# Feed-forward borders rearranged, and the up stage's weight sums made by VectorE

## The chip, the cores and the metric

The kernel runs on one core of a Trainium2 chip. The metric is the device time of one execution in microseconds (us): 1914.89, the median of 3 runs (1914.2 to 1916.0). The core has TensorE (PE), VectorE (DVE), ScalarE (ACT), GpSimd (POOL) and SyncE (SP); here SP issues nearly all transfers.

## The reference

One transformer block over x (2048 x 1024, float32): a mixer (windowed attention with sinks beside a gated spatial unit) and a SwiGLU feed-forward, each between two RMS norms. The change touches the border between the two and the feed-forward (D_FF is 2816):

```python
        mix = jnp.concatenate([rms_norm(a_out, norm_out_attn[l]),
                               rms_norm(s_out, norm_out_sgu[l])], axis=-1) @ w_out[l]
        x = x + rms_norm(mix, norm_mix_post[l])
        f = swiglu(rms_norm(x, norm_ffn_pre[l]), w_gate[l], w_up[l], w_down[l])
        x = x + rms_norm(f, norm_ffn_post[l])
```
with `swiglu(h, ...) = (silu(h @ w_gate) * (h @ w_up)) @ w_down`.

## The kernel before, in words

Every float32 matrix product is made of three matmuls on split operands: hi is the operand rounded (ACT, a copy into float32r), lo is the rest (DVE, raw minus hi). PE needs both splits of both operands.

The kernel goes through four stages, in tiles of 128 rows: the input projection with the mixer (16 tiles), the output projection with both norms (`tile2`, 16 tiles, numbered 0 to 15), the up stage, the down stage.

**Up stage.** The rows come as two blocks of 1024. For each block, 11 groups of 256 columns of D_FF; each group has two halves, u=0 (gate) and u=1 (up). A half is a Strassen-like scheme (Winograd's): 7 products instead of 8, each of 12 matmuls of 512 columns, accumulated in the PSUM banks T0, T1, ZA, ZB, S. Its operands are seven sums of quadrants of the activations (`s_raw`, `s_hi`, `s_lo` 0 to 6, resident for a block, reloaded at the switch to the second block) and eight quadrants or sums of quadrants of the weights (`t_raw`, `t_hi`, `t_lo`, two buffers). Of the weights four quadrants are loaded; the other four (R3, R1, R2, R4) are sums, made before by `t_sums` on POOL. Half n (n = 2g+u) then goes through: `copies` (ACT: p1, p5), `chain` (DVE: u2, u3), `corner` (POOL: v22 = u3 + p5), `upper` and `lower` (DVE: v12, v21), tanh (ACT), `silu` (DVE), and for u=1 `gated` and four sums of the activations (DVE), stored by `act_store` to `act_d` for the down stage. PE's product 7 of a half waits for u3.

**Down stage.** 7 products by 8 row pieces (m = 0 to 7): product `it` is 33 matmuls, with activations `sb_raw` loaded from `act_d` (m 0 to 3 are of the first block) and weights `tb_raw`, which for the second of the seven (i=1) are sums of three quadrants w11 - w01 + w00, made by DVE in `tb_work` with `tb_sub` loads.

**What sets the order.** Nothing is scheduled: every engine does its instructions in the order in which its function in the file is written, and waits on semaphores. A wait at the head of an engine's queue holds all behind it; so does one on SP for the transfers behind it. The functions are `tile2` of each engine, `group` of ACT, DVE and POOL, `up_half` of PE, and the loops of SP. Semaphores that matter: `prod_done` (7 per half), `s_split` and `t_split` (DVE's lo parts, that PE waits for), `tsum_done`, `act_sums`, `act_out`, `sb_split`, `dn_done`.

## Time and profile before

| | |
|---|---|
| median of 3 runs | 1914.89 us |
| the profiled execution | 1916.53 us |
| its span, first to last instruction | 1914.7 us |
| PE busy | 1866.1 us (97%) |
| DVE busy | 1177.1 us (61%) |
| ACT busy | 711.8 us (37%) |
| POOL busy | 565.2 us (30%) |
| mean granted TensorE clock | 0.995 |

The page gives times in us. The output projection ends near 618, the up stage runs from 620 to 1480, the down stage to the end. Busy time of PE is of pipelined matmuls, whose reported durations overlap: the spacing of their starts tells the rate. In the timelines a square bracket gives the time that the engine was idle before the instruction and what it waited for. Line numbers are those of the kernel before.

### The profile page before, as it was taken

The numbers are of one execution on the slowest core, as the hardware profiler recorded it, in microseconds if no ns is written. First come the engines' busy times: TensorE is split into PE (matmuls) and PEld (weight loads), VectorE is DVE, ScalarE is ACT, GpSimd is POOL, SyncE is SP. The second block draws the span as 40 slices with busy tenths as digits, with TensorE's granted clock in tenths as the row PEclk, the third lists the DMA queues.
The fourth block names the chain that finished last, engine by engine and source line by source line (L and its number), as shares of the span: only waits on it lengthen the run. The fifth ranks groups of instructions, "written<-read, shape, count | busy, mean of one in ns | idle before, by whom it ended". The sixth has DMA issues, their size and how long they took to land. (4 is left out here: it accounts for less than half of the span.)

```text
span 1914.7 us, 25262 instructions
## 1 busy us (share of the span) xinstructions
PE 1866.1 (97%) x9464; PEld 1545.5 (81%) x9464; DVE 1177.1 (61%) x1289; ACT 711.8 (37%) x1171; POOL 565.2 (30%) x406
## 2 busy tenths in 40 slices
PE   7999999989999899999999899999999899999998
PEld 5888888878888788888888688888887788888887
DVE  5444444464546877677767867677767556553564
ACT  6555555453335432323234332323333122232342
POOL 2222222220002444444444444444443000000243
PEclk9999999999999999999999999999999999999999
DMA  7111111044575434233426333233324853445655
GB/s 275 67 67 66 66 66 55 33 182 176 207 275 184 171 102 128 90 101 98 129 82 216 125 109 116 82 104 108 117 82 151 323 224 119 164 185 175 230 202 197
DMA packets 129110, 270.27 MB, mean 141 GB/s; under 512 B 5936, under 2 KB 84784, under 8 KB 119600
## 3 DMA queue, kind: packets, MB, share of 16 engines
q1 hardware_dynamic: 129072, 269.78, 40.5%
q8 instruction: 21, 0.34, 0.1%
q14 instruction: 17, 0.14, 0.0%
HBM read 189.54 MB, written 80.22 MB: 141 GB/s over the span
## 5 line engine op out<-in xcount | busy, mean ns | idle before, releaser
L1248 PE MATMUL T<-tb_hi,sb_hi 128*128 128x512 f32 x616 | 240.8, 391 | 7.1 <-DVE sb_lo L1145 7.1
L1250 PE MATMUL T<-tb_hi,sb_lo 128*128 128x512 f32 x616 | 240.2, 390 | 0.0
L1249 PE MATMUL T<-tb_lo,sb_hi 128*128 128x512 f32 x616 | 240.2, 390 | 0.0
L1030 DVE TENSOR_TENSOR t_lo<-t_raw,t_hi 128x1536 fp32r<-128x1536 f32 x132 | 223.9, 1750 | 0.0
L811 ACT ACTIVATE sb_hi<-sb_raw 128x1408 fp32r<-128x1408 f32 x56 | 77.4, 1382 | 299.2 <-PE T L1250 261.1
L575 POOL TENSOR_TENSOR v<-u,p 128x512 f32<-128x512 f32 x44 | 116.3, 2643 | 180.0 <-DVE u L1054 158.0
L559 POOL TENSOR_TENSOR t_raw<-t_raw 128x512 f32<-128x512 f32 x44 | 62.5, 1420 | 280.8 <-DMA t_raw<-w_gu 280.8
L1425 PE MATMUL T<-s_hi,t_hi 128*128 128x512 f32 x352 | 138.7, 394 | 6.7 <-DVE s_lo L1023 4.9
L1248 PEld LDWEIGHTS T<-tb_hi,sb_hi 128*128 128x128 f32 x616 | 116.0, 188 | 33.0 <-issue 8.2
L1427 PE MATMUL T<-s_hi,t_lo 128*128 128x512 f32 x352 | 138.4, 393 | 0.0
L1426 PE MATMUL T<-s_lo,t_hi 128*128 128x512 f32 x352 | 138.1, 392 | 0.0
L1425 PE MATMUL ZB<-s_hi,t_hi 128*128 128x512 f32 x352 | 136.9, 389 | 0.0
L1426 PE MATMUL ZB<-s_lo,t_hi 128*128 128x512 f32 x352 | 136.9, 389 | 0.0
L1427 PE MATMUL ZB<-s_hi,t_lo 128*128 128x512 f32 x352 | 136.9, 389 | 0.0
L1249 PEld LDWEIGHTS T<-tb_lo,sb_hi 128*128 128x128 f32 x616 | 116.0, 188 | 24.2
L1250 PEld LDWEIGHTS T<-tb_hi,sb_lo 128*128 128x128 f32 x616 | 115.9, 188 | 24.1
L1145 DVE TENSOR_TENSOR sb_lo<-sb_raw,sb_hi 128x1408 fp32r<-128x1408 f32 x56 | 96.2, 1718 | 51.5 <-ACT sb_hi L811 51.5
L760 ACT ACTIVATE th<-v 128x512 f32<-128x512 f32 x66 | 41.8, 633 | 215.6 <-POOL v L575 117.5
L599 POOL TENSOR_TENSOR rstdf<-msf,mhalf 128x1 f32<-128x1 f32 x16 | 14.5, 909 | 358.9 <-ACT msf L820 356.7
L1425 PE MATMUL ZA<-s_hi,t_hi 128*128 128x512 f32 x264 | 104.5, 396 | 4.7 <-DVE u L1054 3.2
L1248 PE MATMUL ZB<-wg_hi,hT_hi 128*128 128x512 f32 x256 | 103.1, 403 | 1.6 <-DVE wg_lo L979 1.6
L753 ACT ACTIVATE p<-T 128x512 f32<-128x512 f32 x22 | 13.1, 596 | 244.4 <-PE T L1427 244.4
(199 smaller groups left out, 4614.1 us busy)
## 6 DMA issues: line engine op xcount, KB each, us to landing
t_raw<-w_gu SPq DMA_DIRECT2D x44, 1024.0 KB, 4.8
act_d<-ac SPq DMA_DIRECT2D x22, 1792.0 KB, 8.0
sb_raw<-act_d SPq DMA_DIRECT2D x56, 704.0 KB, 4.1
h_d<-quarters SPq DMA_DIRECT2D x8, 1792.0 KB, 6.6
s_raw<-h_d SPq DMA_DIRECT2D x14, 1024.0 KB, 8.2
tb_raw<-w_dn SPq DMA_DIRECT2D x6, 1536.0 KB, 6.3
hT_raw<-x_t SPq DMA_DIRECT2D x16, 512.0 KB, 3.3
xt<-x SPq DMA_DIRECT2D x16, 512.0 KB, 3.8
```

The source lines that it names most:

```text
L559: e.tensor_tensor(t[:, R3, :], t[:, B22, :], t[:, B12, :], ALU.subtract).then_inc(tsum_done, 1)
L575: e.tensor_tensor(v22[:, :], u3[:, :], p5[:, :], ALU.add).then_inc(v22_done, 1)
L760: e.activation(th[i][:, :], src, ACT.Tanh, scale=0.5).then_inc(th_done, 1)
L811: e.activation(sb_hi[it % 2][:, :, :], sb_raw[it % 2][:, :, :], ACT.Copy).then_inc(sb_hi_done, 1)
L1030: e.tensor_tensor(t_lo[u][:, first:end, :], t_raw[u][:, first:end, :], t_hi[u][:, first - 1:end - 1, :].bitcast(F32), ALU.subtract).then_i ...
L1145: e.tensor_tensor(sb_lo[it % 2][:, :, :], sb_raw[it % 2][:, :, :], sb_hi[it % 2][:, :, :].bitcast(F32), ALU.subtract).then_inc(sb_split, 1)
L1248: e.matmul(out_ap, lhi, rhi, start=start, stop=False)
L1249: e.matmul(out_ap, lhi, rlo, start=False, stop=False)
L1250: return e.matmul(out_ap, llo, rhi, start=False, stop=stop)
L1425: e.matmul(bank, hi, s_hi[i][:, :, w], start=i < 4 and k == 0, stop=False, skip_group_check=True)
L1426: e.matmul(bank, hi, s_lo[i][:, :, w], start=False, stop=False, skip_group_check=True)
L1427: ins = e.matmul(bank, lo, s_hi[i][:, :, w], start=False, stop=k == HK - 1, skip_group_check=True)
```

## The change

**1. Weight sums.** `t_sums` moves from POOL to DVE, unchanged, and stands right ahead of the work that reads it. POOL keeps `corner`.

**2. Entry to the up stage.** The splits of the first three activation sums and the first weights' sums and splits, which stood in or after tile 14, go into tiles 12, 13 and 14 on ACT and DVE. The last tile's transposes move on PE from behind product 2 to behind product 4 of the first half. `chain` stands ahead of the splits 5 and 6, and the last activation sums of the layer before (`pair_sums`) behind the second weights' splits. `silu` writes to a tile of its own, `sil`, and no longer to `ac`, so that it doesn't wait for the last store of `quarters`. DVE at the entry, before, from the first splits on (`s_lo0` to `s_lo6` are the lo parts; `ytmp`, `xres1`, `h2n` are the last tile's norm; `quarters` the pair sums):

```order
L1023 TENSOR_TENSOR s_lo0_130<-s_raw0_116,s_hi0_123 128x2048
L1023 TENSOR_TENSOR s_lo1_131<-s_raw1_117,s_hi1_124 128x2048
L1030 TENSOR_TENSOR t_lo0_139<-t_raw0_137,t_hi0_141 128x1536
L1030 TENSOR_TENSOR t_lo0_139<-t_raw0_137,t_hi0_141 128x1024 x2
L1023 TENSOR_TENSOR s_lo2_132<-s_raw2_118,s_hi2_125 128x2048
L1008 SCALAR_TENSOR_TENSOR ytmp_110<-ZB,rstdm_200,postm_112 128x1024
L1012 TENSOR_TENSOR xres1_109<-ytmp_110,xres1_109 128x1024
L1018 SCALAR_TENSOR_TENSOR h2n_114<-xres1_109,rstdy_203,pref_113 128x1024
L1023 TENSOR_TENSOR s_lo3_133<-s_raw3_119,s_hi3_126 128x2048
L1023 TENSOR_TENSOR s_lo4_134<-s_raw4_120,s_hi4_127 128x2048
```

And now, from the last tile's norm on; the splits 0 to 2 and `t_lo0` stand further up, and the pair sums further down:

```order
L1013 SCALAR_TENSOR_TENSOR ytmp_110<-ZB,rstdm_201,postm_112 128x1024
L1017 TENSOR_TENSOR xres1_109<-ytmp_110,xres1_109 128x1024
L1023 SCALAR_TENSOR_TENSOR h2n_114<-xres1_109,rstdy_204,pref_113 128x1024
L1028 TENSOR_TENSOR s_lo3_133<-s_raw3_119,s_hi3_126 128x2048
L1028 TENSOR_TENSOR s_lo4_134<-s_raw4_120,s_hi4_127 128x2048
L1063 TENSOR_TENSOR u2_147<-ZA,p1_145 128x512
L1068 TENSOR_TENSOR u3_148<-ZA,u2_147 128x512
L1028 TENSOR_TENSOR s_lo5_135<-s_raw5_121,s_hi5_128 128x2048
L1028 TENSOR_TENSOR s_lo6_136<-s_raw6_122,s_hi6_129 128x2048
L1034 TENSOR_TENSOR t_raw1_138<-t_raw1_138 128x512
L1035 TENSOR_TENSOR t_raw1_138<-t_raw1_138 128x512
```

The norm of the last tile has nothing of the splits in front of it any more, and `u2`, `u3` stand two splits earlier.

**3. Switch of blocks.** Splits 4, 5 and 6 are made ahead of the activation sums, and these (`gated_end`) behind the weights' splits. DVE before, from split 3 on (`v21` and `ac` are the end of the last group, `u2`, `u3` the first chain of the new block, with `L1081` to `L1086` the four activation sums):

```order
L1023 TENSOR_TENSOR s_lo3_133<-s_raw3_119,s_hi3_126 128x2048
L1062 TENSOR_TENSOR v21_150<-S,u2_147 128x512
L1070 SCALAR_TENSOR_TENSOR ac_152<-ac_152,v21_150 128x512
L1023 TENSOR_TENSOR s_lo4_134<-s_raw4_120,s_hi4_127 128x2048
L1023 TENSOR_TENSOR s_lo5_135<-s_raw5_121,s_hi5_128 128x2048
L1023 TENSOR_TENSOR s_lo6_136<-s_raw6_122,s_hi6_129 128x2048
L1081 TENSOR_TENSOR ac_152<-ac_152 128x512
L1082 TENSOR_TENSOR ac_152<-ac_152 128x512
L1084 TENSOR_TENSOR ac_152<-ac_152 128x512
L1086 TENSOR_TENSOR ac_152<-ac_152 128x512
L1049 TENSOR_TENSOR u2_147<-ZA,p1_145 128x512
L1054 TENSOR_TENSOR u3_148<-ZA,u2_147 128x512
```

And now:

```order
L1028 TENSOR_TENSOR s_lo2_132<-s_raw2_118,s_hi2_125 128x2048
L1028 TENSOR_TENSOR s_lo3_133<-s_raw3_119,s_hi3_126 128x2048
L1072 TENSOR_TENSOR v12_149<-ZB,u2_147 128x512
L1084 SCALAR_TENSOR_TENSOR ac_152<-sil_153,v12_149 128x512
L1076 TENSOR_TENSOR v21_150<-S,u2_147 128x512
L1028 TENSOR_TENSOR s_lo4_134<-s_raw4_120,s_hi4_127 128x2048
L1028 TENSOR_TENSOR s_lo5_135<-s_raw5_121,s_hi5_128 128x2048
L1028 TENSOR_TENSOR s_lo6_136<-s_raw6_122,s_hi6_129 128x2048
L1063 TENSOR_TENSOR u2_147<-ZA,p1_145 128x512
L1068 TENSOR_TENSOR u3_148<-ZA,u2_147 128x512
L1034 TENSOR_TENSOR t_raw1_138<-t_raw1_138 128x512
```

`v21`'s gated product and the four sums are gone from in front of `u2` and `u3`; behind `u3` come four weight sums (two are shown), then `t_lo1`.

**4. Start of the down stage.** SP issues the third activation load ahead of the last `act_store`, and waits for that store only ahead of the fifth. The weights of i=1 are made without one of their two `tb_sub` loads: DVE adds back the first weights from their hi and lo parts (`add_back`, two passes more). SP before, from the second activation load on (`sb_raw0`, `sb_raw1` are the activation loads, `act_d` the store):

```order
L423 DMA sb_raw1_162<-act_d 128x1408
L356 DMA act_d<-ac_152 3584x1x128
L423 DMA sb_raw0_161<-act_d 128x1408
L414 DMA tb_raw1_154<-w_dn 128x3072
L417 DMA tb_sub1_156<-w_dn 128x3072
L423 DMA sb_raw1_162<-act_d 128x1408
L414 DMA tb_raw1_154<-w_dn 128x2560
L417 DMA tb_sub1_156<-w_dn 128x2560
L423 DMA sb_raw0_161<-act_d 128x1408
L459 DMA postf_168<-post_ffn 128x1024
```

And now:

```order
L426 DMA sb_raw1_163<-act_d 128x1408
L426 DMA sb_raw0_162<-act_d 128x1408
L357 DMA act_d<-ac_152 3584x1x128
L426 DMA sb_raw1_163<-act_d 128x1408
L417 DMA tb_raw1_155<-w_dn 128x3072
L426 DMA sb_raw0_162<-act_d 128x1408
L417 DMA tb_raw1_155<-w_dn 128x2560
L426 DMA sb_raw1_163<-act_d 128x1408
L420 DMA tb_sub1_157<-w_dn 128x3072
L426 DMA sb_raw0_162<-act_d 128x1408
```

The load of `sb_raw0` and the store have changed places; the `tb_sub1` loads stand later and only once each.

The core of the diff:

```diff
 # SP
+            load_t(2)
             h2_store(TILES // 2 - 1)
...
                         load_s(1, 6)
+                        load_t(2 * g + 2)
                     act_store(g - 1)
-                if g + 1 < GROUPS:
+                if g and g != NG and g + 1 < GROUPS:
                     load_t(2 * g + 2)
...
-            act_store(GROUPS - 1)
             e.wait_ge(prod_done, 14 * GROUPS)
             for it in range(7 * TILES // 2):
                 i, m = it // (TILES // 2), it % (TILES // 2)
+                if it + 2 == BP:
+                    e.wait_ge(act_out, 16 * GROUPS)
                 if it + 2 < 7 * TILES // 2:
                     load_sb(it + 2)
...
+                if it == 0:
+                    act_store(GROUPS - 1)
                 if i == 0:
-                    if m < 2:
-                        load_tb(1, 1, 1, m)
-                        load_sub(1, 0, 1, m)
+                    if m in (1, 2):
+                        load_tb(1, 1, 1, m - 1)
                     if m in (3, 4):
-                        e.wait_ge(tb_sum, m - 2)
-                        load_sub(1, 0, 0, m - 3)
+                        load_sub(1, 0, 1, m - 3)
 # POOL, group
-                    if not (last and u and b + 1 == NB):
-                        t_sums(2 * g + u + 1, 1 - u)
                     corner(2 * g + u, g, u)
 # DVE, tile2 (ACT has the hi parts at the same places)
+                if split == 1:
+                    s_lo_part(0, 0)
+                if split == 2:
+                    s_lo_part(0, 1)
+                    s_lo_part(0, 2)
+                if split == 3:
+                    t_sums(0, 0)
+                    t_lo_parts(0, 0)
                 e.wait_ge(rstdm_ready, k + 1)
...
+            for k in range(TILES - 4, TILES - 1):
+                tile2(k // 2, k % 2, 2, 0, True, k - TILES + 5)
 # DVE, group
-                    pair_sums(TILES // 2 - 1)
+                elif first:
+                    s_lo_part(b, 5)
+                    s_lo_part(b, 6)
+                    e.wait_ge(v21_done, n)
+                else:
+                    lower(n - 1, 1)
+                    gated_end(g - 1)
+                if not first:
+                    t_sums(n + 1, 1)
+                chain(n, 0)
+                if begin:
                     s_lo_part(0, 5)
                     s_lo_part(0, 6)
-                else:
-                    group_end(g - 1, b if first else 0)
-                chain(n, 0)
+                if first:
+                    t_sums(n + 1, 1)
                 t_lo_parts(n + 1, 1)
                 if begin:
-                    e.wait_ge(h2_out, 8 * TILES)
+                    pair_sums(TILES // 2 - 1)
+                if first and not begin:
+                    gated_end(g - 1)
...
                 silu(4 * g + 4, 0, 1, v21[:, :])
+                if not final:
+                    t_sums(n + 2, 0)
                 chain(n + 1, 1)
...
+            def add_back(c, n):
+                e.wait_ge(tb_in[2 + c], 16)
+                if n:
+                    e.wait_ge(tb_sum, 3 * c + n)
+                e.tensor_tensor(tb_raw[1][:, half[c], :], tb_raw[1][:, half[c], :],
+                                (tb_hi, tb_lo)[n][0][:, half[c], :].bitcast(F32), ALU.add).then_inc(tb_sum, 1)
 # PE
-                    if begin and u == 0 and i == 1:
+                    if begin and u == 0 and i == 3:
                         h2_transposes(TILES - 1)
```

## Rows read from the trace of the kernel before

**Rows 1.** Busy time by stretch (PE, PEld, DVE, ACT, POOL; instructions; clock; DMA).
```profile
974.60:1012.70 38.10, 38.10 (x169) 31.55 (x169) 27.11 (x27) 11.42 (x14) 16.99 (x10) 1.00 0.33 104
...
617.90:651.00 33.10, 25.51 (x94) 20.05 (x94) 30.71 (x20) 16.46 (x21) 14.68 (x7) 0.85 0.68 261
...
1050.90:1079.70 28.80, 21.86 (x85) 16.48 (x85) 28.61 (x21) 11.22 (x10) 12.45 (x5) 0.94 0.43 147
...
1479.60:1519.20 39.60, 32.48 (x133) 25.47 (x132) 19.30 (x20) 4.45 (x5) 0.00 (x0) 0.96 0.78 300
```

**Rows 2.** Waits of PE: total us, times, longest us.
```profile
PE T L1248 <- DVE sb_lo L1145: 7.1, 4, 5.4
...
PE T L1425 <- DVE s_lo L1023: 4.9, 3, 2.7
...
PE ZA L1425 <- DVE u L1054: 3.2, 1, 3.2
...
PE S L1375 <- DVE h2n L1018: 3.1, 1, 3.1
...
PE T L1425 <- DVE t_lo L1030: 1.8, 1, 1.8
...
PE ZA L1425 <- DVE s_lo L1023: 1.6, 1, 1.6
```

**Rows 3.** Timeline of PE, entry to the up stage (start, us, operation, [idle before]).
```profile
621.92 0.63 PE L1426 MATMUL T<-s_lo,t_hi 128*128 128x512 f32 x1
...
622.34 0.63 PE L1427 MATMUL T<-s_hi,t_lo 128*128 128x512 f32 x1
...
643.76 0.50 PE L1425 MATMUL T<-s_hi,t_hi 128*128 128x512 f32 x1 [2.66 <-DVE s_lo L1023]
...
650.98 0.39 PE L1425 MATMUL ZB<-s_hi,t_hi 128*128 128x512 f32 x1
```

**Rows 4.** Same stretch: SP's timeline, landing times of s_raw, ACT's timeline.
```profile
617.12 1.29 SPq L347 DMA_DIRECT2D s_raw<-h_d  x2
...
DMA to landing us min/median/max: 7.8/11.7/15.5
...
635.38 1.92 ACT L724 ACTIVATE s_hi<-s_raw 128x2048 fp32r<-128x2048 f32 x1 [0.66 <-DMA s_raw<-h_d]
```

**Rows 5.** Timelines of DVE and POOL, in steady groups and at the entry.
```profile
977.07 1.78 DVE L1082 TENSOR_TENSOR ac<-ac 128x512 f32<-128x512 f32 x1
...
996.05 1.30 POOL L559 TENSOR_TENSOR t_raw<-t_raw 128x512 f32<-128x512 f32 x1 [6.65 <-DMA t_raw<-w_gu]
...
1002.15 0.69 DVE L1049 TENSOR_TENSOR u<-S,p 128x512 f32<-128x512 f32 x1 [4.26 <-PE S L1427]
...
617.99 4.02 DVE L1030 TENSOR_TENSOR t_lo<-t_raw,t_hi 128x1536 fp32r<-128x1536 f32 x3
...
641.42 4.49 DVE L1023 TENSOR_TENSOR s_lo<-s_raw,s_hi 128x2048 fp32r<-128x2048 f32 x2
```

**Rows 6.** Timelines of ACT and PE at the switch of blocks.
```profile
1059.72 1.91 ACT L724 ACTIVATE s_hi<-s_raw 128x2048 fp32r<-128x2048 f32 x1 [3.14 <-DMA s_raw<-h_d]
...
1075.58 0.77 PE L1425 MATMUL ZA<-s_hi,t_hi 128*128 128x512 f32 x1 [3.15 <-DVE u L1054]
```

**Rows 7.** Timelines of SP, ACT, PE at the down stage's start; DVE by form.
```profile
1487.46 0.52 SPq L356 DMA_DIRECT2D act_d<-ac  x1
...
1488.09 4.48 SPq L423 DMA_DIRECT2D sb_raw<-act_d  x1
...
1499.02 1.38 ACT L811 ACTIVATE sb_hi<-sb_raw 128x1408 fp32r<-128x1408 f32 x1 [19.20 <-DMA sb_raw<-act_d]
...
1502.18 0.79 PE L1248 MATMUL T<-tb_hi,sb_hi 128*128 128x512 f32 x1 [5.38 <-DVE sb_lo L1145]
...
L1145 DVE TENSOR_TENSOR sb_lo<-sb_raw,sb_hi 128x1408 fp32r<-128x1408 f32 x56 | 96.2, 1718 | 51.5 <-ACT sb_hi L811 51.5
...
L1152 DVE TENSOR_TENSOR tb_raw<-tb_raw,tb_sub 128x3072 f32<-128x3072 f32 x4 | 13.4, 3351 | 0.0
```

More of the change, by code:

```diff
@@ L584, in _ @@
             tile2(0, 1, 1, 0, True)
-            with e.Fori(1, TILES // 2 - 1) as j:
+            with e.Fori(1, TILES // 2 - 2) as j:
                 for par in range(2):
                     tile2(j, par, 2, 0, True)
-            t_sums(0, 0)
+            for par in range(2):
+                tile2(TILES // 2 - 2, par, 2, 0, True)
             tile2(TILES // 2 - 1, 0, 2, 0, False)
@@ L701, in quarter_copies, with tile2 @@
                         .then_inc(quarter_done, 1)
-            def tile2(j, par, before, last, ahead):
+            def tile2(j, par, before, last, ahead, split=0):
                 k = 2 * j + par
@@ L766, in group @@
                     s_hi_part(0, 4)
-                    quarter_copies(TILES - 1, 0, True)
-                    s_hi_part(0, 5)
-                    s_hi_part(0, 6)
-                    for p in range(2):
-                        e.wait_ge(x1_out[p], 8 * TILES)
                     e.wait_ge(h2n_done, TILES)
@@ L776, in group @@
                 copies(n, 0)
+                if first and b == 0:
+                    s_hi_part(0, 5)
+                    s_hi_part(0, 6)
+                    quarter_copies(TILES - 1, 0, True)
+                    for p in range(2):
+                        e.wait_ge(x1_out[p], 8 * TILES)
                 t_hi_parts(n + 1, 1)
@@ L839, in _ @@
                     sb_hi_part(it + 1)
-                if m in (5, 6) and i < 6:
-                    c = m - 5
-                    if i < 4:
-                        e.wait_ge(tb_sum, (4, 6, 10, 12)[i] - 1 + c)
+                if m in (5, 6 if i else 7) and i < 6:
+                    c = m // 6
+                    if i == 0:
+                        e.wait_ge(tb_sum, 3 + 3 * c)
+                    elif i < 4:
+                        e.wait_ge(tb_sum, (8, 12, 14)[i - 1] - 1 + c)
                     else:
@@ L1001, in pair_sums, with tile2 @@
                 e.tensor_tensor(q[:, 7, :], q[:, 2, :], q[:, 5, :], ALU.subtract).then_inc(sums_done, 1)
-            def tile2(j, par, before, last, ahead):
+            def tile2(j, par, before, last, ahead, split=0):
                 k = 2 * j + par
@@ L1034, in _ @@
             tile2(0, 1, 1, 0, True)
-            with e.Fori(1, TILES // 2 - 1) as j:
+            with e.Fori(1, TILES // 2 - 2) as j:
                 for par in range(2):
                     tile2(j, par, 2, 0, True)
-            tile2(TILES // 2 - 1, 0, 2, 0, False)
-            s_lo_part(0, 0)
-            s_lo_part(0, 1)
-            t_lo_parts(0, 0)
-            s_lo_part(0, 2)
+            for k in range(TILES - 4, TILES - 1):
+                tile2(k // 2, k % 2, 2, 0, True, k - TILES + 5)
             tile2(TILES // 2 - 1, 1, 2, 1, False)
@@ L1065, in silu, with gated_start, upper_end, gated_end @@
                 e.wait_ge(th_done, count)
-                e.scalar_tensor_tensor(out=ac[:, slot, :], in0=th[i][:, :], scalar=1.0, in1=src,
+                e.scalar_tensor_tensor(out=sil[:, slot, :], in0=th[i][:, :], scalar=1.0, in1=src,
                                        op0=ALU.add, op1=ALU.mult).then_inc(sil_done, 1)
             def gated(slot, src):
-                e.scalar_tensor_tensor(out=ac[:, slot, :], in0=ac[:, slot, :], scalar=0.5, in1=src,
+                e.scalar_tensor_tensor(out=ac[:, slot, :], in0=sil[:, slot, :], scalar=0.5, in1=src,
                                        op0=ALU.mult, op1=ALU.mult).then_inc(act_done, 1)
-            def group_end(g, next_block):
-                lower(2 * g + 1, 1)
+            def gated_start(g):
+                e.wait_ge(sil_done, 4 * g + 4)
+                e.wait_ge(v22_done, 2 * g + 2)
+                gated(3, v22[:, :])
+                e.wait_ge(prod_done, 14 * g + 12)
+                gated(1, GU[1][0])
+            def upper_end(g):
+                upper(2 * g + 1, 1)
+                e.wait_ge(v12_done, 2 * g + 2)
+                gated(2, v12[:, :])
+            def gated_end(g):
                 e.wait_ge(v21_done, 2 * g + 2)
                 gated(0, v21[:, :])
-                if next_block:
-                    for i in range(4, 7):
-                        s_lo_part(next_block, i)
                 e.wait_ge(act_done, 4 * g + 4)
@@ L1403, in up_half @@
                 for i, (s, t) in enumerate(UP_PRODUCTS):
-                    if i == 0 and not begin:
-                        e.wait_ge((sil_done, act_done)[u], 4 * g)
+                    if not begin and i == 0:
+                        e.wait_ge((sil_done, act_done)[u], 4 * g - 2)
+                    if not begin and i in (1, 3):
+                        e.wait_ge((v12_done, v21_done)[i // 2], n - 1)
                     if i < 3:
```

96 lines of the change are left out of this document (53 added, 43 removed).

## The prediction

> **What bounds the kernel now.** I read the page's busy table first, then the waits of PE, then busy time by stretch, and last the timelines of the engines around the places where PE waits. PE is busy 97% of the span, so a change that leaves the matmuls alone can win at most what PE idles, plus what the idling costs in clock. A group in the middle of the up stage shows that its steady part has nothing to give: PE is busy 38.1 of 38.1 us, at full clock, while DVE works 27.1 us and POOL 17.0 us [rows 1]. At 168 matmuls in 38.1 us a matmul takes 0.227 us, a product (12 of them) 2.72 us, a half of a group (7 products) 19.05 us. What PE waits for around the feed-forward borders is six rows of the waits [rows 2]: 7.1 + 4.9 + 3.2 + 3.1 + 1.8 + 1.6 = 21.7 us. They lie in three stretches: A, the entry into the up stage (617.9 to 651.0), B, the switch to the second block (1050.9 to 1079.7), C, the first products of the down stage (1479.6 to 1519.2) [rows 1].
>
> After some waits PE also runs at the lower clock level (1.2 GHz for 2.4): starts lie 0.42 us apart where 0.227 is usual, 621.92 and 622.34 for instance [rows 3], and the granted clock of stretch A is 0.85 [rows 1]. A and B and C hold five such runs, of 8 matmuls each: 8 x 0.2 = 1.6 us per run, 8 us in all. It followed the waits of 1.8, 3.1, 2.7, 3.2 and 5.4 us and did not follow some others of 1.4 to 2.0 us. The ceiling of the change is so 21.7 + 8 = 29.7 us. The Trainium skill (TensorE: Matmul & The Clock Gate, What's actually happening) says that the gate follows how busy the array has been, not the length of one wait; by that rule each wait that is left may or may not bring a run, which is 1.6 us either way. Without that page I charge a run to each left wait over 2.5 us and keep 1.6 us of doubt at A and at B.
>
> **Steady groups: the weight sums go from POOL to DVE.** Per group eight sums leave POOL and eight 128x512 operations join DVE. Such an operation takes 0.68 us by itself, 0.6 start to start, and 1.78 us where a POOL sum runs beside it [rows 5]. So DVE pays 8 x 0.6 = 4.8 us and gets back three activation sums' 1.1 us and one activation's 0.9: about 4.2. It ends near 27.7 us of 38.1 and stays hidden. Order matters more than load, since DVE now stands at the head of its own queue waiting for the weights. In the half shown, the weights land at 996.05 (POOL starts then), DVE is free at 997.0, the sums end at 999.5, and DVE's next work for PE comes at 1002.15 after 4.26 us of idling [rows 5]. The low parts behind it need be there at 1012.7 and have some 4.7 us of slack. Term: 0. If that cover were gone, a late microsecond would cost 20 groups one each (rival 3). The Trainium skill (Perfetto Trace Analysis, Optimizing Scalar/DVE Operations) warns that moving operations between GpSimd and DVE may not help, since they share a read port. By that rule DVE is no better or worse off than before, where plain addition would put it at 31.9 us; the rows above agree with it to 0.6 us, and by either DVE stays under 38.1.
>
> **Border A.** Before, the last attention matrix products and their transposes end at 617.96. PE waits 1.8 us for the weights' low parts, 3.1 for the last normalized tile, 2.7 for a split (643.76), and starts the second half at 650.98 [rows 2, 3]: 33.0 us for work of 7 x 2.72 + 0.9 = 19.9. The change moves the splits of the first three quadrants and the weights' sums and splits into tiles 12 to 14 on ACT and DVE, where both idle some 5 us per tile. The heaviest tile (14) carries four sums (2.5 us) and three low parts (4.0 [rows 5]): 1.4 us over the cover, taken up by the end of the tile. So PE starts at 617.96, and the last tile's normalization comes near 625 and not at 630, ahead of its transposes, which now stand behind the fourth product. What is late next is the fourth quadrant. Its load is issued at 617.12 after the last attention product, which the change leaves, and lands 7.8 us later, at 624.9 [rows 4]. ACT's split takes 1.9, DVE's 2.24 [rows 4, 5]: 629.2. PE is there at 617.96 + 3 x 2.72 = 626.1 and waits 3.1 us, and pays one clock run. Its half then ends at 629.2 + 1.6 + 4 x 2.72 + 0.9 = 642.6. The seventh quadrant lands at 635.4 [rows 4]; with its splits DVE is at 639.6, four sums of 0.61 make 642.1, the first low part 643.7. So the second half starts at 643.8, bound by DMA and DVE. POOL's corner add and the store of the last tile, 5 us earlier among the loads, can each put off up to 1.1 us; I take 0.7. Gain of A: 651.0 - 644.5 = 6.5 us. Bounds: 8 if the store costs nothing and no clock run comes, 4 if the loads land 1.3 us later and the second wait brings a run.
>
> **Border B.** Before, the first half of the second block takes 1050.9 to 1079.7 [rows 1], 28.8 us for 19.05. The last wait (3.15 us at 1075.58 [rows 6]) is on u3, queued on DVE behind three splits and four activation sums. Now DVE does, from 1054.1, splits 2 and 3 (to 1058.5), three small operations (1060.4), splits 4, 5, 6 (2.2 each, to 1067.0; the seventh high part is there at 1059.72 + 1.9 [rows 6]), u2 and u3 (1068.4), four weight sums, and the first low part. PE's fourth product starts on time (1059.4), the fifth at 1062.7 (0.6 late), the seventh at 1068.5 (0.4 late), ending at 1071.2. The weight sums end at 1070.9, or 1072.0 with POOL's corner add beside them (1.1 us [rows 5]), the low part at 1073.6: the sums that POOL used to do ahead of time now stand behind u3, a new wait of 2.5 us. The second half starts at 1073.7. Gain 1079.7 - 1073.7 = 6.0; half a clock run off: 5.2. Bounds 3.5 and 7.
>
> **Border C.** Before, the store of the last activations is issued at 1487.46 and the third activation load behind it at 1488.09; that load lands 10.9 us later, ACT had sat idle 19.2 us for it, and PE waited 5.4 us to 1502.18 with a clock run after it [rows 7]. Now the load is issued ahead of the store, at 1481, when DVE is done with the first split. Even at 10.9 us it lands at 1492, and its two splits, 1.4 on ACT and 1.7 on DVE [rows 7], end before 1496.8, where PE wants them. Next is the fourth load. It stands behind the store, issued at 1489.0, when the second split is done; at the 10.9 us of its like it lands at 1500, and PE, three products of 7.5 us in, wants the splits at 1504.3, so the load by 1501.2. Of the 7.1 us of waits on the activation splits [rows 2] the first (1.4, behind DVE's weight splits, which don't move) and one of 0.2 stay: 7.1 - 1.6 + 1.6 for the run = 7.1 us of gain. The change also moves one pair of weight loads less and makes two more DVE passes over the new weights, 3.35 us for the wide form [rows 7] and 2.8 for the narrow one. Followed through its own queue, DVE has their last low part at 1541.2; eight products from 1481.1 on end at 1541.7, where PE needs it (before, at 1549.4, some 8 us after it was there). This 0.5 us is the thinnest margin of the change. Bounds: 4 (fourth load 1.5 us late, with a run) and 8.
>
> **Sum.** 6.5 + 5.2 + 7.1 = 18.8 us. The profiled execution took 1916.53 us (span 1914.7), so 1897.7 for it; the median of the timed runs is 1914.89, 1.6 below it, which gives 1896.1.
>
> **Rivals.**
> 1. Only C comes through. The waits of A and B that were behind queued work come back as waits on loads (fourth and seventh quadrant in A) and on the weight sums, which POOL used to make ahead of time. For it speak the two new waits worked out above; against it that each is shorter than what it takes the place of. Time: 1914.9 - 7.1 = 1907.8.
> 2. C's margins fail: the fourth load is late by 1.8 us and brings a run, and the new weights are 2 us late, again with a run. For it: with more in flight the load's like took longer than it may here. Cost 7 us: 1903.
> 3. Slower. DVE, waiting at the head of its queue for a weight load, sends the low parts late in every steady group. It decides from the point where loads land over 4.7 us later than at 996.05, or where the sums meet POOL at 1.78 us each (8 x 1.2 = 9.4 us more in a group). At 1.2 us per group, 20 groups cost 24 us: 1896.1 + 24 = 1920. Against it: 10 us of DVE's group are free, and POOL has little left that could meet the sums.
> 4. The moved splits in tiles 12 to 14 hold up what the attention stage needs, and tile 14's 1.4 us shows on PE: A is zero or less, 1903.
>
> **How the numbers follow.** Forecast 0.65, rival 1 0.10, rival 2 0.11, rival 3 0.06, rival 4 0.04; 0.04 for a stall that I don't see and that eats the gain. A difference shows from 0.2%, 3.8 us. The forecast's own bounds are 11.5 (4 + 3.5 + 4) to 23 us (8 + 7 + 8) of gain; with rivals 2 and 4 inside, the range is 1889 to 1905. Faster takes the forecast and rivals 1, 2 and 4, less 0.01 for their tails: 0.89; same 0.05, slower 0.06.
>
> **What would show it.** Right: PE starts the up stage within 0.3 us of the last transposes; the wait for u in stretch B is gone, and one of 1 to 3 us for t_lo is there in A and in B; no wait over 1 us for sb_lo but the first, of 1.4; DVE busy 27 to 28.5 us in a steady group, PE 38.1. Wrong: PE waits inside steady groups, a wait for tb_lo at the ninth down product, or one of over 4 us for the fourth quadrant.

## The result, and the profile after

| | median | runs | ratio to before, 95% interval |
|---|---|---|---|
| before, on the same chip | 1915.16 us | 4 | |
| changed | 1900.77 us | 4 (1900.31 to 1901.72) | 0.9924 [0.9909, 0.9939] |
| changed, run once more later | 1901.60 us | 5 (1900.32 to 1902.29) | 0.9923 [0.9909, 0.9936] |

The change makes the kernel 14.4 us faster; 18.8 were forecast. The time lies 4.7 us over the forecast and inside its range. The profiled execution took 1901.72 us, with a span of 1899.9.

The waits of PE in the changed kernel, to be held against [rows 2] (total us, times, longest us):

```profile
PE ZA L1298 <- DVE wq_lo L976: 11.5, 3, 9.5
PE ZA L1477 <- DVE s_lo L1028: 4.3, 1, 4.3
PE ZB L1477 <- DVE t_lo L1047: 3.6, 2, 2.6
...
PE T L1298 <- DVE sb_lo L1184: 1.6, 2, 1.4
PE T L1477 <- DVE s_lo L1028: 1.3, 2, 0.8
```

The last four rows are what is left of the borders' 21.7 us: 10.8. The waits for u and for h2n are gone. The first row is the start of the program, which the change doesn't touch; it was 10.3 us in the profile before, so this execution was about 1 us late when it came to the change. Markers further on are therefore compared as differences within a stretch.

Busy time by stretch (PE, PEld, DVE, ACT, POOL; clock; DMA share; GB/s): a steady group, the entry A, the switch B, the down stage's start C, beside [rows 1]:

```profile
967.30:1005.40 38.10, 38.10 (x169) 31.56 (x169) 28.18 (x35) 11.32 (x14) 5.30 (x2) 1.00 0.32 103
618.80:647.10 28.30, 22.29 (x94) 17.42 (x92) 19.52 (x15) 16.95 (x21) 2.37 (x3) 0.94 0.74 270
1047.20:1070.60 23.40, 20.10 (x86) 15.51 (x85) 23.10 (x19) 11.09 (x10) 1.61 (x1) 1.00 0.45 172
1473.60:1511.10 37.50, 37.24 (x163) 30.58 (x164) 26.69 (x22) 5.53 (x4) 0.00 (x0) 1.00 0.86 320
```

The steady group takes 38.1 us as before, with DVE at 28.2 for 27.1 and POOL at 5.3 for 17.0. A shrinks from 33.1 to 28.3 us. B's first half shrinks from 28.8 to 23.4 us, and DVE is busy for 23.1 of them: B is now DVE's. C keeps PE busy throughout.

PE's timeline at the three borders (start, us, operation, [idle before]):

```profile
618.77 0.47 PE L1477 MATMUL T<-s_hi,t_hi 128*128 128x512 f32 x1
...
631.55 0.80 PE L1477 MATMUL ZA<-s_hi,t_hi 128*128 128x512 f32 x1 [4.33 <-DVE s_lo L1028]
...
647.12 0.50 PE L1477 MATMUL ZB<-s_hi,t_hi 128*128 128x512 f32 x1 [0.92 <-DVE t_lo L1047]
...
1047.25 0.47 PE L1477 MATMUL T<-s_hi,t_hi 128*128 128x512 f32 x1
...
1070.58 0.47 PE L1477 MATMUL ZB<-s_hi,t_hi 128*128 128x512 f32 x1 [2.64 <-DVE t_lo L1047]
...
1077.73 0.39 PE L1477 MATMUL S<-s_hi,t_hi 128*128 128x512 f32 x1
...
1473.64 0.47 PE L1298 MATMUL T<-tb_hi,sb_hi 128*128 128x512 f32 x1 [1.35 <-DVE sb_lo L1184]
```

The difference to before, stretch by stretch:
- **A**: from PE's entry (617.96 before, 618.77 now) to the second half (650.98 in [rows 3], 647.12): 33.0 against 28.35 us, 4.7 us gained. Forecast 6.5.
- **B**: the first half of the new block takes 23.3 us for 28.8, 5.5 us gained. But the product behind it took 5.44 us for two before and takes 7.15 now (1070.58 to 1077.73): its matmuls begin at the lower clock level, starts 0.42 us apart. That leaves 3.75. Forecast 5.2.
- **C**: the first down product starts at 1473.64 where before it started at 1481.07, 7.43 earlier; the whole span is 14.8 us shorter, so 7.4 us come after that point. Forecast 7.1. From this point to the end the span has 426.2 to 426.4 us in all nine profiles of kernels with the new start of the down stage, and 433.4 to 433.6 in the four without it.

The three add up to 15.9 us and the two profiled executions differ by 14.8: 0.8 of the rest is the later arrival at the up stage, and 0.2 lies between the stretches.

### The profile page after: what moved, and what is told of

The parts are those of the page before. It is cut to its first block and busy times, and to the rows that moved or that the text cites. A ratio compares the mean times of both kernels' runs of the same rounds, so it can differ in the third digit from the quotient of the medians.

```text
span 1899.9 us, 25241 instructions
## 1 busy us (share of the span) xinstructions
PE 1860.3 (98%) x9464; PEld 1542.3 (81%) x9464; DVE 1210.2 (64%) x1467; ACT 710.3 (37%) x1171; POOL 294.3 (15%) x230
## 5 line engine op out<-in xcount | busy, mean ns | idle before, releaser
L1478 PE MATMUL ZA<-s_lo,t_hi 128*128 128x512 f32 x264 | 103.3, 391 | 0.0
L1479 PE MATMUL ZA<-s_hi,t_lo 128*128 128x512 f32 x264 | 103.2, 391 | 0.0
```

Of the source, the lines that this page charges most:

```text
L1478: e.matmul(bank, hi, s_lo[i][:, :, w], start=False, stop=False, skip_group_check=True)
L1479: ins = e.matmul(bank, lo, s_hi[i][:, :, w], start=False, stop=k == HK - 1, skip_group_check=True)
```

## The experiments

All were timed beside the kernel before. Run times of the kernel before on the three chips used have medians of 1915.73, 1915.93 and 1916.09 us.

### Only the down stage's start

The kernel before with the change's part at the down stage alone:

```
-            act_store(GROUPS - 1)
...
+                if it + 2 == BP:
+                    e.wait_ge(act_out, 16 * GROUPS)
                 if it + 2 < 7 * TILES // 2:
                     load_sb(it + 2)
...
+                if it == 0:
+                    act_store(GROUPS - 1)
                 if i == 0:
-                    if m < 2:
-                        load_tb(1, 1, 1, m)
-                        load_sub(1, 0, 1, m)
+                    if m in (1, 2):
+                        load_tb(1, 1, 1, m - 1)
...
+            def add_back(c, n):
```

> The kernel before with only the change at the start of the down stage: third activation load ahead of the last store, and the new weights made with add_back. Theory (the borders add up, each by its own waits): the 5.4 us wait and its clock run go, 7.1 us of gain, 1908 us; the third down product starts without a wait. Rival (the gain needs the freer GpSimd and DVE of the whole change): under 4 us, 1911 or more, with a wait of 2 us or more left at the third or fourth product.

Measured: 1907.82 us (5 runs, 1907.49 to 1908.72), ratio 0.9959 [0.9945, 0.9972], 7.9 us faster. Its wait on the activation splits:

```profile
PE T L1261 <- DVE sb_lo L1147: 1.5, 2, 1.3
```

So C alone is worth what was charged to it, and needs nothing of A and B.

### Only the up stage's part

The changed kernel with the down stage's start put back as it was, the reverse of the diff above.

> The changed kernel with the down stage's start put back as before. Theory: what is left of the gain is that of entry and switch, some 7.5 us by the two traces (4.8 + 3.7, less 1.1 that both traces' starts differ by), 1907 to 1908 us, and the 5.4 us wait is back. Rival (the entry and the switch gain nothing on the clock, all is from the down stage): 1913 or more.

Measured: 1907.78 us (5 runs, 1907.26 to 1909.09), ratio 0.9958 [0.9944, 0.9972], 8.0 us faster, where A and B were forecast at 11.7. The shortfall is thus in A and B. The two parts add up to 15.9 us against 14.3 to 14.4 together; with medians that move by 0.5 to 1 us between chips I can't say whether that difference is real.

### Only the third load ahead of the store

The kernel before with the store behind the third activation load and the weight loads left as they were, with both loads for the subtraction:

```
             load_sb(1)
-            act_store(GROUPS - 1)
...
+                if it + 2 == BP:
+                    e.wait_ge(act_out, 16 * GROUPS)
                 if it + 2 < 7 * TILES // 2:
                     load_sb(it + 2)
...
+                if it == 0:
+                    act_store(GROUPS - 1)
...
-                        e.wait_ge(act_out, 16 * GROUPS)
```

> The kernel before with the third activation load issued ahead of the last store, and nothing else of the change: both weight subtrahends are still loaded. Theory (the issue order is what frees the third load; the saved transfer only guards the fourth): 4 to 7 us of gain, 1908 to 1911; the third product without a wait, the fourth or fifth perhaps with one of up to 2 us, since 1.5 MB more are in flight. Rival (the saved transfer matters most): under 3 us.

Measured: 1915.81 us (11 runs, 1914.94 to 1918.7), ratio 1.0 [0.9991, 1.0009]: no gain. My theory was wrong. SP's timeline in it, then the wait on ACT, then on PE:

```profile
1488.61 0.52 SPq L356 DMA_DIRECT2D act_d<-ac  x1
1489.17 4.44 SPq L414 DMA_DIRECT2D tb_raw<-w_dn  x1
1493.66 1.23 SPq L417 DMA_DIRECT2D tb_sub<-w_dn  x1
1494.93 0.70 SPq L423 DMA_DIRECT2D sb_raw<-act_d  x1
...
1507.57 1.38 ACT L813 ACTIVATE sb_hi<-sb_raw 128x1408 fp32r<-128x1408 f32 x1 [16.13 <-DMA sb_raw<-act_d]
...
1510.65 0.80 PE L1250 MATMUL T<-tb_hi,sb_hi 128*128 128x512 f32 x1 [5.23 <-DVE sb_lo L1147]
```

The third load is in time, and the same wait (5.2 us for 5.4) has moved to the fourth product. Its load is issued at 1494.93 behind the store and two weight loads and its split starts 12.6 us later. In the changed kernel (SP, then ACT) nothing stands between the store and the fourth activation load:

```profile
1466.88 7.01 SPq L426 DMA_DIRECT2D sb_raw<-act_d  x2
1480.03 0.52 SPq L357 DMA_DIRECT2D act_d<-ac  x1
1481.56 3.47 SPq L426 DMA_DIRECT2D sb_raw<-act_d  x1
1485.08 1.23 SPq L417 DMA_DIRECT2D tb_raw<-w_dn  x1
...
1491.41 1.38 ACT L806 ACTIVATE sb_hi<-sb_raw 128x1408 fp32r<-128x1408 f32 x1 [8.56 <-DMA sb_raw<-act_d]
```

Here the third load is the second of the two from 1466.88 on, the fourth is issued at 1481.56, and its split starts 9.85 us later (1491.41), well ahead of about 1496.4, at which PE gets there (1473.64 and three products of 7.6 us). So the order of store and load gains nothing without what the change does to the weight loads: it issues them later, and one transfer less. Which of these two does more was not tried, nor what they give with the old order.

### The weight sums back on GpSimd

The changed kernel with `t_sums` on POOL, where the kernel before has it:

```
@@ POOL, group
+                    if not (last and u and b + 1 == NB):
+                        t_sums(2 * g + u + 1, 1 - u)
                     corner(2 * g + u, g, u)
@@ DVE, group (and the same ahead of the other splits)
-                if not first:
-                    t_sums(n + 1, 1)
                 chain(n, 0)
```

> The changed kernel with the weight sums put back on GpSimd, at their old places in its queue, all else as changed. Theory (moving the sums is worth nothing in steady groups, and at the switch GpSimd made them ahead of time but at 1.1 us of DVE each): within 2 us of the changed kernel, 1899 to 1903; steady groups at 38.1 us either way. At the switch the wait for the low parts of the second half changes by at most 2 us from 2.6. Rival A (the move costs: DVE's new work behind u3 is the wait of 2.6 us and its clock run): 3 us or more faster than the changed kernel, 1897. Rival B (the move is the main gain, the shared port freed): 4 us or more slower, 1905.

Measured: 1910.14 us (6 runs, 1907.6 to 1911.1), ratio 0.9966 [0.9954, 0.9978], 5.6 us faster than before and 8.5 to 9.4 slower than the changed kernel. My theory was wrong; the time is that of rival B. Steady groups are not where it goes: PE is at 38.10 of 38.10 us there. First two of PE's waits, neither of which the changed kernel has; then the timelines of DVE, POOL and PE at the switch:

```profile
PE ZB L1473 <- ACT p L762: 6.4, 2, 3.5
...
PE ZA L1473 <- DVE u L1070: 1.8, 1, 1.8
```
```profile
1061.49 9.39 DVE L1042 TENSOR_TENSOR s_lo<-s_raw,s_hi 128x2048 fp32r<-128x2048 f32 x3
...
1072.18 6.21 DVE L1049 TENSOR_TENSOR t_lo<-t_raw,t_hi 128x1536 fp32r<-128x1536 f32 x3
1078.32 1.78 DVE L1086 SCALAR_TENSOR_TENSOR ac<-sil,v 128x512 f32<-128x512 f32 x1
...
1062.21 3.23 POOL L565 TENSOR_TENSOR t_raw<-t_raw 128x512 f32<-128x512 f32 x1
...
1089.81 0.80 PE L1473 MATMUL ZB<-s_hi,t_hi 128*128 128x512 f32 x1 [3.53 <-ACT p L762]
```

And DVE at the same place in the changed kernel:

```profile
1056.76 6.69 DVE L1028 TENSOR_TENSOR s_lo<-s_raw,s_hi 128x2048 fp32r<-128x2048 f32 x3
...
1064.74 0.68 DVE L1034 TENSOR_TENSOR t_raw<-t_raw 128x512 f32<-128x512 f32 x1
1065.34 1.78 DVE L1035 TENSOR_TENSOR t_raw<-t_raw 128x512 f32<-128x512 f32 x1
...
1068.68 4.03 DVE L1047 TENSOR_TENSOR t_lo<-t_raw,t_hi 128x1536 fp32r<-128x1536 f32 x3
```

With POOL's sums beside them, three splits take 9.39 us for 6.69 and three low parts 6.21 for 4.03; a POOL sum that takes 1.30 us alone [rows 5] takes up to 3.23. DVE has four sums less to do here, and so is only 1.3 us later than in the changed kernel at the end of the low parts, counted from the block's first product (26.8 us for 25.5). But its next five operations, the gated product and the four activation sums, take 6.4 us for 3.3 beside POOL's next four sums, and it comes to the gate's next operation 4.5 us late (33.1 us for 28.6). ACT's copies come last in that chain: PE stops once more, four products into the second half, in both blocks (2.83 us at 660.76 and 3.53 at 1089.81), and starts each time at the lower clock level. These two stops are the whole difference: from A's end to the switch PE takes 4.6 us more than in the changed kernel and from there to the down stage 5.0, while A is as long (28.1 us). It is not that POOL does its corner behind the sums: ACT's tanh, which needs the corner, is done at 1075.8, and DVE comes for it at 1084.74.

### The sums on VectorE alone

The kernel before, with `t_sums` moved to DVE and nothing else:

```
@@ DVE, entry
             tile2(TILES // 2 - 1, 0, 2, 0, False)
+            t_sums(0, 0)
             s_lo_part(0, 0)
@@ DVE, group
+                if not first:
+                    t_sums(n + 1, 1)
                 chain(n, 0)
+                if first:
+                    t_sums(n + 1, 1)
...
+                if not final:
+                    t_sums(n + 2, 0)
                 chain(n + 1, 1)
```

> The kernel before with one part of the change alone: the sums of the weight quadrants made by VectorE where the changed kernel makes them; borders, loads and the down stage's start as before. The changed kernel with the sums back on GpSimd took 1910.1, 8.5 to 9.4 us more than with them on VectorE. Theory 1 (the sums beside VectorE's splits are slow whatever the border looks like, so the part is worth something alone): 1911 to 1914, with the splits ahead of the switch's u and t_lo at 2.24 us each and not 3.1. Theory 2 (what they cost arises where the new border has VectorE's splits just ahead of TensorE's need; before, the same lateness falls into waits that other things end): 1915 to 1916, no change. Rival (VectorE gets 2.5 us more work in each product pair and is late at the old borders): 1917 or more.

Measured: 1917.86 us (11 runs, 1915.29 to 1919.94), ratio 1.001 [1.0001, 1.0019], 1.8 us slower if anything. It lies on the rival's side, and not far enough from theory 2 to count it out; theory 1 is false. The profile has both signs. At the switch it gains 2.1 us: from the block's first product to the product that starts the second pair 32.1 us (1053.34 to 1085.46) for 34.2. At the entry it loses, since four sums now stand in DVE's queue ahead of the first splits (start, us, DVE and then PE):

```profile
614.07 0.68 DVE L1014 TENSOR_TENSOR t_raw<-t_raw 128x512 f32<-128x512 f32 x1
...
616.72 4.49 DVE L1008 TENSOR_TENSOR s_lo<-s_raw,s_hi 128x2048 fp32r<-128x2048 f32 x2
621.12 4.02 DVE L1027 TENSOR_TENSOR t_lo<-t_raw,t_hi 128x1536 fp32r<-128x1536 f32 x3
...
622.93 0.79 PE L1429 MATMUL T<-s_hi,t_hi 128*128 128x512 f32 x1 [4.49 <-DVE t_lo L1027]
...
651.64 0.50 PE L1429 MATMUL ZB<-s_hi,t_hi 128*128 128x512 f32 x1 [2.47 <-DVE t_lo L1027]
```

PE waits 4.5 us for t_lo where it waited 1.8 [rows 2], but that by itself hardly shows: the second half starts 33.2 us after PE's entry for 33.0. The loss is behind it. There PE waits 2.5 us for the next t_lo, behind four more sums, and goes on at the lower clock level, so that the second pair of products starts 40.4 us after the entry for 38.5: 1.9 us. The two profiled executions are so within 0.4 us of each other, and the 1.8 us between the medians stand in neither. So this part alone is worth nothing and, beside the new borders, 8.5 to 9.4 us. The parts of the change can't be priced one at a time.

### What A lacks: the last load of x

In the changed kernel SP issues the last tile's load of x behind two stores of tile 14, which wait for DVE. DVE with the entry's work in its queue is late there. SP, DVE and ACT at the entry of the changed kernel, and the landing times of s_raw (the first, of the fourth quadrant, is the shortest):

```profile
614.76 0.32 SPq L345 DMA_DIRECT2D h_d<-quarters  x1
615.18 0.38 SPq L379 DMA_DIRECT2D xres<-x  x1
618.17 1.41 SPq L348 DMA_DIRECT2D s_raw<-h_d  x2
...
624.57 1.22 DVE L1017 TENSOR_TENSOR xres<-ytmp,xres 128x1024 f32<-128x1024 f32 x1 [3.11 <-DMA xres<-x]
...
627.94 1.28 DVE L1023 SCALAR_TENSOR_TENSOR h2n<-xres,rstdy,pref 128x1024 f32<-128x1024 f32 x1 [2.14 <-POOL rstdy L556]
629.20 2.29 DVE L1028 TENSOR_TENSOR s_lo<-s_raw,s_hi 128x2048 fp32r<-128x2048 f32 x1
...
627.26 1.91 ACT L721 ACTIVATE s_hi<-s_raw 128x2048 fp32r<-128x2048 f32 x1
...
DMA to landing us min/median/max: 9.1/13.0/16.7
```

Two things end together at ACT's split of the fourth quadrant (627.26). ACT is done with the last tile's norm at 627.21, and the quadrant's own load, issued at 618.17, lands 9.1 us later, at 627.3; before the change it took 7.8 [rows 4]. Both hang on the x load: the norm needs it, and the quadrant's load lands 2.7 to 2.8 us behind it in this profile and in five others with this border. Either one alone would have held the split as long. With the weight sums back on GpSimd, ACT even stood idle 1.2 us for this transfer. The experiment issues that load ahead of the stores. It was timed with the two that follow it and, for comparison on one chip, the changed kernel as it is:

> The changed kernel once more, on the same chip as the three below. Every theory: 1900 to 1901 us.

The edit:

```
+                def load_xres():
...
+                if k == TILES - 2:
+                    load_xres()
                 e.wait_ge(x1_done, k + 1)
                 e.dma_start(x1_d[rows(k), :], xres[par][:, :]).then_inc(x1_out[par], 16)
                 if k:
                     if par == 0:
                         h2_store(j - 1)
-                    if k < TILES - 1:
...
+                    if k < TILES - 2:
+                        load_xres()
```

> The changed kernel with the load of the last tile of x (for xres) issued ahead of tile 14's stores, some 13 us sooner. In the changed kernel DVE waits 3.1 us for that load, and the split of the fourth quadrant comes at 629.2 behind the last normalization. Theory 1 (the fourth quadrant's own load is as late, landing at 627.3, and binds): the DVE wait goes, but PE's wait of 4.3 us at the fourth product shrinks by 0.5 to 1.5 us only, what 0.5 MB less in flight gives; 0.5 to 1.5 us of gain. Theory 2 (the queue behind the late norm binds): the wait falls to 1.5 us or less and its clock run goes, 3 to 4 us of gain.

Measured: 1898.98 us (5 runs, 1898.35 to 1900.04), ratio 0.9912 [0.9898, 0.9925]; the changed kernel on the same chip took 1901.60, 0.9923 [0.9909, 0.9936], and the two sets of runs don't overlap. In its trace:

```profile
625.16 1.92 ACT L725 ACTIVATE s_hi<-s_raw 128x2048 fp32r<-128x2048 f32 x1 [1.28 <-DMA s_raw<-h_d]
...
629.45 0.50 PE L1481 MATMUL ZA<-s_hi,t_hi 128*128 128x512 f32 x1 [2.57 <-DVE s_lo L1032]
...
645.31 0.50 PE L1481 MATMUL ZB<-s_hi,t_hi 128*128 128x512 f32 x1 [1.15 <-DVE t_lo L1051]
```

Now the transfer ends the wait, which is 2.6 us for 4.3 and 4.0, and lands 7.3 us after its issue. A takes 26.9 us from the up stage's first matmul (618.43) for 28.35 and, in the profile from the same chip, 28.6. The forecast's figure for this was 643.8 + 0.7 - 617.96 = 26.5. Neither theory has it whole: the transfer binds and the wait shrinks by 1.4 to 1.8 us, near what theory 1 says, but the gain is above its range; and the stretch at the lower clock level behind the wait stays, against theory 2. Of the 3.2 us between the two profiled executions 1.7 are A's. The other 1.6 are the pair of products behind the wait for t_lo at the switch, 5.6 us for 7.1: the wait is 2.6 us in both, but here no stretch at the lower clock level follows it. Nothing ties that to the load, so of the 2.6 us between the medians only A's part is shown to be its work.

### Two small ones: the first subtraction ahead of its turn

DVE's first subtraction for the new block is put between the two operations of the chain, with ACT's part ahead of the weights' splits:

```
-            def chain(n, u):
+            def chain(n, u, between=None):
...
+                if between:
+                    between()
                 e.wait_ge(prod_done, 7 * n + 4)
...
-                chain(n + 1, 1)
+                chain(n + 1, 1, (lambda: s_lo_part(b + 1, 0)) if switch else None)
@@ ACT, group
+                if last and b + 1 < NB:
+                    s_hi_part(b + 1, 0)
                 if not (last and b + 1 == NB):
                     t_hi_parts(n + 2, 0)
```

> The changed kernel with one split moved at the switch of blocks: high part of the new block's first quadrant ahead of the weights' on ACT, and its low part on DVE between u2 and u3 of the last half, where DVE idles 2.0 us. Theory (DVE's queue from 1044.8 to 1070.4 binds the second half's start): the wait of 2.6 us for the low parts falls by 1 to 2 us; if what is left brings no clock run, the gain is 2.5 to 3.5 us, else 1 to 1.5. Rival (the wait is bound by the seventh quadrant's load or ACT's copies): no change in that wait.

Measured: 1901.04 us (5 runs, 1899.46 to 1902.39), ratio 0.992 [0.9906, 0.9933]. From the block's first product to the second pair's start B takes 29.8 us for 30.5 in the changed kernel's second profile. But the wait for t_lo itself is 2.58 us for 2.64, where the theory had it fall by 1 to 2: that is the rival's sign. PE comes to it 0.7 us sooner, and DVE's low parts are ready 0.7 us sooner as well. The time, 0.6 us lower, is within the spread of the runs.

The same with `tb_lo_part(0, 0)` for the first down product:

```
-                chain(n + 1, 1)
+                chain(n + 1, 1, (lambda: tb_lo_part(0, 0)) if final else None)
...
-                    tb_lo_part(0, 0)
                     tb_lo_part(0, 1)
```

> The changed kernel with the first low part of the down weights between u2 and u3 of the last half, not behind u3. Theory (the first down product waits for DVE's queue: two weight splits and one activation split from 1464.8 to 1473.4): the 1.35 us wait goes, since 1.5 to 2 us of the split lie in DVE's idle time before u3; 1.3 us of gain, and the margin at the ninth product, 0.3 us, is not touched. Rival (u3 late by 1.5 us holds PE's seventh product): no gain, a new wait for u.

Measured: 1901.25 us (5 runs, 1900.87 to 1902.57), ratio 0.9924 [0.9911, 0.9938]. The wait of 1.35 us is gone from the profile, where the down stage starts 394.4 us after the second block's second pair of products for 395.9. The time is 0.35 us lower, which tells nothing.

### The transposes back behind the second product

```
-                    if begin and u == 0 and i == 3:
+                    if begin and u == 0 and i == 1:
                         h2_transposes(TILES - 1)
```

> The changed kernel with the last tile's transposes back behind the second product of the up stage, where they stood before; all else as changed. They then wait for h2n of the last tile, which the changed kernel's trace has at 627.94 to 629.2, and the third and fourth product stand behind them. Theory (the transposes' old place cost TensorE its wait for h2n a second time): products one to three end at 627.2 in the changed kernel and the fourth starts at 631.55; with the transposes in between the fourth can start at 629.3 + 1.6 for eight transposes + 1.7 to 2 for the third product, 632.8 to 633: 1.3 us later, 1902.9 to 1903. Rival (the fourth product waits for s_lo anyway, which the transposes' place does not move): within 0.4 us of the changed kernel, 1901.6.

Measured: 1902.12 us (5 runs, 1900.96 to 1904.15), ratio 0.9933 [0.9919, 0.9946]. PE waits for h2n, behind the second product, and does the third and fourth after it:

```profile
628.36 1.97 PE L1425 MATMUL S<-ident,h2n 128*128 128x128 f32 x8 [4.61 <-DVE h2n L1023]
...
647.93 0.50 PE L1477 MATMUL ZB<-s_hi,t_hi 128*128 128x512 f32 x1 [1.41 <-DVE t_lo L1047]
```

A takes 29.9 us (618.02 to 647.93) for 28.35 and 28.6 in the two profiles of the changed kernel, the 1.3 that the theory gives. The median is 0.5 to 1.4 us higher, which fits the theory but doesn't exclude the rival.

### All three improvements together

The three edits of the early load, the switch and the down stage's start in one kernel.

> The changed kernel with three edits together: the last load of x issued ahead of tile 14's stores, DVE's first subtraction for the new block put between the two operations of the chain ahead of it, and at the down stage's start the first small subtraction put between the same two. Singly they gave 1899.0, 1901.0 and 1901.3 where the changed kernel gave 1901.6, so 2.6, 0.6 and 0.3 us. Theory (they lie on three different waits of TensorE, so they add): 3.5 us, 1898 us, at most 1898.6. Rival (one late step behind takes the gain of the earlier ones back, or the small ones were noise): 1899.0 to 1901. PE's waits of over 0.9 us in the feed-forward part should be 2.6 for s_lo and 2.6 for t_lo, and none for sb_lo.

Measured: 1897.84 us (4 runs, 1897.24 to 1899.03), ratio 0.9907 [0.9892, 0.9922], 18.25 us faster than before and 3.8 more than the changed kernel, where the single gains add up to 3.55. This agrees with the theory; since the two small ones were within the spread of the runs, it doesn't show what each gives. The waits of PE left at the borders are as expected 2.6 us for s_lo and 2.6 for t_lo, and none over 0.3 for sb_lo; beside them stand one of 1.3 for s_lo and one of 1.4 for t_lo in A, which the theory did not have. In this profile the wait of 2.6 us for s_lo in A brings no stretch at the lower clock level.

## Why the prediction was right, and where it was off

**Steady groups, term 0: right.** PE stays at 38.10 us in a group, DVE at 28.2, inside the 27 to 28.5 of the text. Rival 3 (1920) did not come: POOL, at 5.3 us a group, no longer meets the sums.

**What the move of the sums is worth: not priced at all.** I took it as neutral and as one more thing ahead of PE at B. The experiments with the sums put back and with the sums alone show that beside the new borders it is 8.5 to 9.4 us, and alone nothing: at the new borders DVE is the bound (23.1 of 23.4 us), and POOL's sums beside it make DVE's operations longer. That the forecast did not suffer is luck of method: it followed DVE's queue with every split at its undisturbed 2.2 us, which is right only because POOL is idle, and it never asked what the sums would cost if they stayed. The Trainium skill (Perfetto Trace Analysis, Optimizing Scalar/DVE Operations) says that moving operations between GpSimd and DVE might not help, since they share a read port. The runs here show more than the sentence says: on DVE the sums cost 0.6 us each, on POOL they stretch three splits by 2.7 us, and the move pays or not by what else is due at that moment.

**A, 6.5 us forecast, 4.7 measured.** That PE starts at once, that the waits for h2n and for t_lo at the entry go and that the fourth quadrant is late next, all came. The step that failed is "The heaviest tile (14) carries four sums (2.5 us) and three low parts (4.0 [rows 5]): 1.4 us over the cover, taken up by the end of the tile". It was not taken up: tile 14's two stores wait for DVE, and SP issues the last x load behind them 3.6 us ahead of PE's entry (615.18 to 618.77), where before it was about 5.0. The forecast has no term for that load. DVE waits 3.1 us for it, so the last tile's norm comes at 627.94 where I had about 625; and the fourth quadrant's load, right behind it, lands 9.1 us after its issue where I had 7.8. The split on ACT is held by both at the same moment; I had priced it from its transfer alone, and that too short. The wait was 4.3 us (4.0 in the second profile) for the 3.1 forecast. A wait of over 4 us for the fourth quadrant stood among my own signs of being wrong, and in the first profile it came. With the load moved ahead, A comes to 26.9 us, within 0.4 of the forecast. That moves the load by some 13 us, so how much the 1.4 us alone cost stays open.

**B, 5.2 us forecast, 3.75 measured.** The queue walk held: the wait for u is gone, one of 2.64 us for t_lo takes its place (I had 2.5), and the first half is 5.5 us shorter (6.0). The mis-sized term is the clock run: I took half of one, 0.8 us, and a whole one came, 7.15 - 5.44 = 1.7 us. Nothing that these profiles show tells when it comes: in the run with the transposes back, the same wait of 2.6 us brought none, the pair of products behind it took 5.5 us and B gained 5.35.

**C, 7.1 forecast, 7.4 measured.** The first wait of 1.35 us stays, no other is over 0.3. The fourth load's split started 9.85 us after the issue, where 10.9 was reckoned for the landing. The thin margin at the ninth product was there as well (DVE, then PE):

```profile
1531.15 2.83 DVE L1179 TENSOR_TENSOR tb_lo<-tb_raw,tb_hi 128x2560 fp32r<-128x2560 f32 x1 [0.28 <-ACT tb_hi L800]
...
1534.30 0.49 PE L1298 MATMUL T<-tb_hi,sb_hi 128*128 128x512 f32 x1
```

The low part ends at 1533.98, 0.3 us ahead of PE; the forecast had 0.5. What the working got wrong is the reason: it credits the order of store and third load and takes the fourth load's 10.9 us as given, without saying that the weight loads must be out of its way; the run with the order alone gained nothing.

**Rivals.** Rival 1 (only C, 1907.8) is what the run without A and B gives, 1907.8, and not what the change did. Rival 2 had the right place: with the weight loads left in, the fourth load does fail, by 5.2 us. Rival 4's mechanism, moved splits that hold up tile 14, is part of A's shortfall, through SP's queue and the x load and not through PE, at no more than the 1.5 to 1.7 us that A gets back with that load moved, and not at the 6.5 us that it was given.

The measured time lies inside the range, 4.2 us from its slow end: the two misses, 1.8 us at A and 1.45 at B, go the same way, and C's 0.3 hardly counts against them.

## What to carry to other kernels

When work is moved into an earlier stage's idle time, follow the moved engine's delay through the queue that issues transfers: a load that stands behind a store that waits for that engine is late with it, and so are the loads behind that one. When two things hold the same instruction at the same moment, taking away one of them gains nothing; look at both before naming the cause. When an engine becomes the bound at a border, look at what its neighbours do at that moment before anything else; an offload that is free in the steady part cost 8.5 to 9.4 us there in this kernel. And a load taken out from behind a store needs the load after it looked at as well, or the wait only moves by one.

## What the runs showed of the hardware

- The lower clock level after a wait is not decided by that wait alone. The wait of 2.6 us for t_lo at the switch stood in eight profiles of kernels with the new border and sums on DVE: a run of 6 or 7 steps of 0.42 to 0.43 us from one matmul start to the next followed in six, none in two. After the s_lo wait at the entry, of 4.3 and 4.0 us, came runs of 6 and 10 such steps in two profiles of the same kernel; with the x load moved ahead that wait was 2.6 us in two profiles, and a run followed in one. One run at the switch cost 1.6 to 1.7 us. Five such runs lay at the borders before, two in the changed kernel's first profile.
- A 128x512 sum on POOL takes 1.30 us alone [rows 5] and 3.23 beside DVE's splits, while three 128x2048 splits on DVE go from 6.69 to 9.39 us: both engines lose.
- A single POOL operation beside a run of DVE operations cost 1.1 us on DVE here (1.78 for 0.68 us, at 1065.34).
- The fourth quadrant's 1 MB load landed 9.1 us after its issue with the x load 3 us ahead of it, and 7.3 with that load long done.
- From the issue of an activation load to the start of the split that waited for it took 9.85 us right behind the store in the changed kernel, 10.9 right behind it before [rows 7], and 12.6 with two weight loads between.
